# Hybrid SSD and sparse-attention layer: the across decay's matmul joined to the segment sums, all y products one unit later

## The chip, the cores and the metric

The program runs on one core of a Trainium2 chip. The metric is device time in microseconds, the median of several runs. A profile of one execution stands beside it; its lines name engines: PE is TensorE (matmul; PEld its weight loads), DVE is VectorE, ACT is ScalarE, POOL is GpSimd, SPq the queue that issues the DMAs.

## The reference

One decoder layer on x (1, 256, 1024). The input is normalised and modulated, multiplied by one wide matrix `w_in`, and split. One branch is a Mamba-2 SSD scan in two chunks of 128 tokens with 32 heads in 4 groups; the other is a sparse attention with 16 heads. Both are projected, gated, summed, projected again and added to x. The part that the change touches is the SSD scan:

```python
a_cs = jnp.cumsum(adt, axis=2)
seg = a_cs[:, :, :, None] - a_cs[:, :, None, :]
decay = jnp.exp(jnp.where(causal, seg, -jnp.inf))
cb = jnp.einsum('bclgn,bcsgn->bclsg', c_, b_)
y_diag = jnp.einsum('bclsg,bclsgh,bcsghp->bclghp', cb, decay, xdt)
...
y_off = jnp.einsum('bclgn,bcghpn,bclgh->bclghp', c_, prev, jnp.exp(a_cs))
return (y_diag + y_off).reshape(bsz, s, h, p)
```

## The kernel before

**Weight units.** All weights come in units of 128x1024 (512 KB), one DMA each into seven `w_raw` slots. `weight_units` fixes their order (133 of them). For a unit, ACT rounds the raw weights to `w_hi` (L955), DVE and for a part of the columns POOL form `w_lo` = raw - hi (L1230, L1574), and PE runs 8 x 3 matmuls of 256 columns (L727 to L729: hi·hi, hi·lo, lo·hi) into one of three gemm banks in PSUM. ACT and DVE then read the bank out. For the x tiles that is a causal convolution: `conv_acc` on ACT (L988), three taps on DVE (L1277), a tanh on ACT (L997), a gate on DVE (L1239, `x_conv_T`). For z tiles it is a tanh (L962) and a gate (L1239). ACT and DVE prepare weights three units ahead of PE (`AHEAD`). The two `native` matrices w1k and w1v (L703) are used without a split; DVE reads their result at L1299 and L1300 (`cmp_hidden`).

**The order.** `schedule` writes by hand which steps follow which unit: `put(u, step)`. PE and POOL walk through `STEPS`: unit u, then the steps put behind it. ACT and DVE walk through `LATE_STEPS`, in which the steps of unit u stand behind the work of unit u+1. Each engine executes its own list in order, and semaphores tie the lists together. In unit numbers, 13 to 44 are the x and z tiles, four x and four z for each of the SSM groups g; 45 to 49, 52, 55 and 58 are tiles of the attention gate, 50, 51, 53, 54 are w1k, and 56, 57, 59, 60 are w1v. Group g's steps are placed from b = 20 + 8g:

- `xt` (g, c), c = 0, 1: four transposes of the convolved x (L774), which DVE scales to `x_dt` (L1425).
- `seg` i, for each quad i = 2g and 2g+1 of four heads: two matmuls of 512 columns into the score banks (L788); ACT applies relu and exp to each (L1126, L1128: `decay`); DVE (L1432) and POOL (L1624) multiply the two chunks by `cb_T` to `cb_decay`.
- `ea` i: one matmul of 512 columns into a small bank (L793) with the same moving rows; ACT takes the exp (L1133, `decay_across`) and then makes the moving rows of the next quad (L1058, `seg_moving`, four instructions); POOL multiplies by `cb_T` to `cb_decay_across` (L1639).
- `y` i: 12 matmuls with 64 output columns each (L813, L816) into the bank `y_or_o`; DVE adds the skip term in two instructions (L1438) and multiplies by the gate (L1443).
- `ysq` g: ACT squares the group's y (L1140); `ysum` g: POOL adds the squares (L1633, L1634); `ssq`: PE sums them over partitions (L823) and ACT takes the root (L1143), which loads another activation table.

Of the kernel before, what the change touches and what calls it, by code (L numbers as in the profile page):

```python
# [82 lines left out]
def schedule():  # L83

    after = {}

    def put(u, *steps):
        after.setdefault(u, []).extend(steps)

    put(len(PAIRS) - 2, ("ada2", 0))
    put(6, ("dtT", 0))  # L100
    put(7, ("dtA", 0), ("dtE", 0))
    put(8, ("dtB", 0), ("dtL", 0))
    put(10, ("dtC", 0))
    put(13, ("acs", 0))
    for kind in range(3):
        put(15 + kind, ("cb", kind))
    for g in range(SSM_GROUPS):
        b = 20 + 8 * g
        put(b, ("xt", (g, 0)))
        put(b + 1, ("xt", (g, 1)), ("seg", 2 * g))  # L110
        put(b + 2, ("ea", 2 * g))
        put(b + 4, ("y", 2 * g), ("seg", 2 * g + 1))
        put(b + 5, ("ea", 2 * g + 1))
        last = g == SSM_GROUPS - 1
        put(b + 7 + last, ("y", 2 * g + 1))
        put(b + 8 + last, ("ysq", g))
        put(b + 10 + last, ("ysum", g))
    for g in range(KV_GROUPS):
        put(18 + 8 * g, ("blk0", g))
        put(19 + 8 * g, ("blk1", g))  # L120
    put(47, ("clear", 0))
    put(48, ("ssq", 0))
    put(58, ("ssq", 1))
    tiles = TPG * SSM_GROUPS
    w1k, w1v, ks, q, mg = (UNITS.index((kind, 0, 0)) for kind in ("w1k", "w1v", "ks", "q", "mg"))
    norm_units = [w1k + 1, w1k + 2, w1k + 4, w1k + 5, w1v + 1, w1v + 2, w1v + 4, ks + 2, ks + 4, q + 1, q + 3, q + 5]
    norm_units += [mg + n for n in (4, 6, 8, 10, 12, 14)]
    for g, u in enumerate((w1k + 1, w1k + 3, ks + 4, ks + 5)):
        put(u, ("rec", g))
    for j in range(tiles + 2):  # L130
        for ahead, name in ((2, "ynlo"), (1, "ynhi"), (0, "yn")):
            if 0 <= j - ahead < tiles:
                put(norm_units[j], (name, j - ahead))
    at = UNITS.index
    put(at(("w1k", 0, 3)) + 2, ("hidT", 0))
    put(at(("w1v", 0, 3)) + 2, ("hidT", 1))
    put(at(("w1v", 0, 3)) + 1, ("kcp", 0))
    put(at(("w1v", 0, 3)) + 5, ("vcp", 0))
    put(at(("vs", 1, 0)) + 2, ("vt", 0))
    put(at(("w1v", 0, 3)) + 3, ("zero", 0))  # L140
    tiles = [u for u, unit in enumerate(UNITS) if unit[0] != "ag"]
    q7 = tiles.index(at(("q", 7, 0)))

    def after_tile(n, *steps):
        put(tiles[n], *steps)

    after_tile(q7 + 1, ("cs", 0), ("cs", 1))
    after_tile(q7 + 3, ("vt", 1))
    after_tile(q7 + 5, ("ct", 0), ("ct", 1))
    t0 = q7 - 2  # L150
    after_tile(t0 - 3, ("kpos", 0))
    for h in range(ATT_HEADS):
        after_tile(t0 - 2 + 2 * h, ("q2", h))
    for n in range(ATT_HEADS + 2):
        for ahead, name in ((0, "sc"), (2, "pt"), (0, "ex"), (1, "ps")):
            if 0 <= n - ahead < ATT_HEADS:
                after_tile(t0 + 2 * n, (name, n - ahead))
    after_tile(q7 + 2, ("cs2", 0))
    last_h = tiles.index(at(("mg", 15, 0)))
    for p in range(ATT_HEADS // 2):  # L160
        after_tile(t0 + 8 + 4 * p + (p == 0), ("pv", p))
        after_tile(max(last_h + 3, t0 + 8 + 4 * p), ("osp", p))
    put(at(("nsa", 4, 0)), ("agB", 0))
    put(at(("nsa", 6, 0)), ("agB", 1))
    steps = []
    for u in range(len(UNITS)):
        steps.append(("gemm", u))
        steps += after.get(u, [])
    steps += [("flush", 0)]

    late = []
    for u in range(len(UNITS)):
        late += [("gemm", u)] + after.get(u - 1, [])
    late += [("flush", 0)] + after.get(len(UNITS) - 1, [])
    return steps, late


STEPS, LATE_STEPS = schedule()
SPLIT_IDX, NATIVE_IDX, TILE_IDX = {}, {}, {}
for _u, (_kind, _j, _part) in enumerate(UNITS):  # L180
# [1611 lines left out]
```

## Time and profile before

| | us |
|---|---|
| median of 3 runs | 454.94 |
| lowest and highest | 454.66 to 456.67 |
| the profiled execution | 455.79 |
| its span in the trace | 454.0 |
| PE busy | 435.1 (96%) |
| DVE busy | 346.3 (76%) |
| ACT busy | 281.5 (62%) |
| POOL busy | 205.6 (45%) |

Times in the views are microseconds from the start of the span. Matmuls are pipelined: the profiler's durations overlap, and the distance between two starts is what one costs in a stream. "Idle before" is the time in which an engine stood still ahead of a group, with what ended it. The granted clock (PEclk) is the share of TensorE's full clock that the chip allowed.

### The profile page before, as it was taken

How to read it: one execution, taken by the hardware profiler on the slowest of the kernel's cores; microseconds unless marked ns; L12 is line 12 of the kernel's file. 1: busy time of each engine (PE TensorE's matmuls, PEld its weight loads, DVE VectorE, ACT ScalarE, POOL GpSimd, SP SyncE). 2: the span in 40 equal slices, each digit the busy share in tenths (PEclk: the TensorE clock that was granted, in tenths of full speed). 3: DMA queues.
4: the chain of work that ended last, by engine and by line, in shares of the span. 5: the costliest groups of instructions: out<-in, count | busy, mean ns of one | idle time of the engine just before them, and what ended most of it. 6: DMA issues, size and time to landing. Idle time of an engine off the chain costs nothing.

```text
span 454.0 us, 9851 instructions
## 1 busy us (share of the span) xinstructions
PE 435.1 (96%) x3638; PEld 400.5 (88%) x3638; DVE 346.3 (76%) x615; ACT 281.5 (62%) x560; POOL 205.6 (45%) x195
## 2 busy tenths in 40 slices
PE   2899999999999999999899999999999999999995
PEld 2597999999999999986899999999989899999873
DVE  0366889999999999468788879478668888787633
ACT  3245885878687986656898647476557554544441
POOL 0147661533346436735483444355443653355430
PEclk9999999999999999999999969999999999999999
DMA  7999636474535436168756442424344364497002
GB/s 283 420 415 397 210 135 186 139 232 141 171 110 167 158 141 184 49 198 274 266 190 214 160 140 95 139 93 152 129 160 165 140 244 176 170 385 249 33 0 92
DMA packets 22391, 84.04 MB, mean 185 GB/s; under 512 B 2492, under 2 KB 2882, under 8 KB 21186
## 3 DMA queue, kind: packets, MB, share of 16 engines
q1 hardware_dynamic: 22344, 83.42, 52.6%
q8 instruction: 29, 0.48, 0.4%
q14 instruction: 18, 0.15, 0.1%
HBM read 82.36 MB, written 1.05 MB: 184 GB/s over the span
## 4 chain that ended last, share of the span: by engine, by line
PE 50%; DVE 1%; issue 0%; ACT 0%; DVEq 0%
PE gemm L727 12%; PE gemm L729 11%; PE gemm L728 11%; PE y_or_o L933 3%; PE score L897 1%; PE score L899 1%; PE small L871 1%; PE score L900 1%; PE small L652 1%; PE small L654 1%; PE score L654 1%; PE score L653 1%; PE small L653 1%; PE score L652 1%; PE small L909 1%; PE small L915 1%
## 5 line engine op out<-in xcount | busy, mean ns | idle before, releaser
L1574 POOL TENSOR_TENSOR w_lo<-w_raw,w_hi 128x256 fp32r<-128x256 f32 x89 | 116.0, 1307 | 159.1 <-ACT w_hi L955 150.6
L727 PE MATMUL gemm<-h_hi,w_hi 128*128 128x256 f32 x600 | 171.5, 286 | 2.1 <-DVE cmp_hidden L1300 1.2
L729 PE MATMUL gemm<-h_hi,w_lo 128*128 128x256 f32 x600 | 167.8, 280 | 0.0
L728 PE MATMUL gemm<-h_lo,w_hi 128*128 128x256 f32 x600 | 167.8, 280 | 0.0
L1230 DVE TENSOR_TENSOR w_lo<-w_raw,w_hi 128x768 fp32r<-128x768 f32 (+1 forms) x117 | 128.1, 1098 | 42.8 <-ACT w_hi L955 42.3
L955 ACT CAST w_hi<-w_raw 128x1024 fp32r<-128x1024 f32 x117 | 122.2, 1045 | 44.8 <-PE gemm L729 25.2
L727 PEld LDWEIGHTS gemm<-h_hi,w_hi 128*128 128x128 f32 x600 | 114.1, 190 | 5.9 <-issue 3.0
L728 PEld LDWEIGHTS gemm<-h_lo,w_hi 128*128 128x128 f32 x600 | 114.3, 191 | 0.8 <-issue 0.2
L729 PEld LDWEIGHTS gemm<-h_hi,w_lo 128*128 128x128 f32 x600 | 113.9, 190 | 0.0
L727 PE MATMUL gemm<-ynorm_hi,w_hi 128*128 128x256 f32 x128 | 36.1, 282 | 0.0
L729 PE MATMUL gemm<-ynorm_hi,w_lo 128*128 128x256 f32 x128 | 35.4, 276 | 0.0
L728 PE MATMUL gemm<-ynorm_lo,w_hi 128*128 128x256 f32 x128 | 35.4, 276 | 0.0
L1624 POOL TENSOR_TENSOR cb_decay<-decay,cb_T 128x512 f32<-128x512 f32 x8 | 14.5, 1816 | 44.7 <-ACT decay L1128 39.1
L1277 DVE SCALAR_TENSOR_TENSOR conv_acc<-gemm,conv_half,conv_acc 128x255 f32<-128x255 f32 (+2 forms) x66 | 31.6, 479 | 3.0 <-ACT conv_acc L988 1.3
L1188 ACT ACTIVATE probs<-score,softmax_small 128x128 f32<-128x128 f32 (+1 forms) x64 | 26.1, 422 | 11.3 <-DVE softmax_small L1493 11.3
L727 PEld LDWEIGHTS gemm<-ynorm_hi,w_hi 128*128 128x128 f32 x128 | 24.0, 188 | 0.7 <-issue 0.7
L728 PEld LDWEIGHTS gemm<-ynorm_lo,w_hi 128*128 128x128 f32 x128 | 24.1, 188 | 0.0
L729 PEld LDWEIGHTS gemm<-ynorm_hi,w_lo 128*128 128x128 f32 x128 | 24.0, 188 | 0.0
L1195 ACT COPY probs_T<-small 128x512 f32<-128x512 f32 x16 | 9.4, 590 | 23.1 <-PE y_or_o L933 21.6
L988 ACT ACTIVATE conv_acc<-gemm,conv_half 128x256 f32<-128x256 f32 x22 | 12.4, 565 | 16.2 <-DVE x_conv_T L1239 8.7
L962 ACT ACTIVATE tanh_tmp<-gemm 128x256 f32<-128x256 f32 x24 | 9.1, 380 | 16.2 <-PE gemm L729 15.3
L727 PE MATMUL gemm<-o_hi,w_hi 128*128 128x256 f32 x64 | 18.8, 294 | 0.0
(253 smaller groups left out, 893.0 us busy)
## 6 DMA issues: line engine op xcount, KB each, us to landing
w_raw<-in_wpack SPq DMA_DIRECT2D x133, 512.0 KB, 3.7
w_ada_shift_scale<-in_w_ada SPq DMA_DIRECT2D x8, 1024.0 KB, 15.5
x_T<-in_xT SPq DMA_DIRECT2D x2, 512.0 KB, 5.9
x_residual<-in_x_tok SPq DMA_DIRECT2D x1, 1024.0 KB, 6.1
out_tok_dram<-out_tok SPq DMA_DIRECT2D x4, 256.0 KB, 2.1
ada_gate_products<-in_gate_bias SPq DMA_DIRECT2D x1, 512.0 KB, 4.0
g_post_rows<-in_g_post_rows SPq DMA_DIRECT2D x1, 512.0 KB, 5.7
consts<-in_consts SPq DMA_DIRECT2D x1, 272.0 KB, 22.0
```

The costliest lines, as they stand in the source:

```text
L727: nc.tensor.matmul(bank[:, 0:SEQ], w_hi, hi[:, k0 + k, :], start=first, stop=False)
L728: nc.tensor.matmul(bank[:, 0:SEQ], w_hi, lo[:, k0 + k, :], start=False, stop=False)
L729: last = nc.tensor.matmul(bank[:, 0:SEQ], w_lo, hi[:, k0 + k, :], start=False, stop=end)
L933: last = nc.tensor.matmul(bank[64 * k:64 * k + 64, P * kt:SEQ], V[:, b, kt, g, :], src, start=False, stop=(b == 1 and kt == 1), skip_group ...
L955: nc.scalar.copy(WH[:, n % HI_SLOTS, :], RAW[:, u % RAW_SLOTS, :]).then_inc(hi_ready, 1)
L988: nc.scalar.activation(ACC[:, ci % 2, :], bank, ACT.Identity, bias=CW[:, 96 + col:97 + col], scale=CW[:, 4 * col + 3:4 * col + 4]).then_in ...
L1188: last = nc.scalar.activation(E[:, k, b, P * qt:P * qt + nk], SB[qt][:, nk * b:nk * b + nk], ACT.Exp, bias=SM[:, k, 0, c:c + 1], accum_out ...
L1195: nc.scalar.copy(PT[:, i % 2, :, 0:SEQ], bank[:, :].rearrange("p (b q) -> p b q", b=2)).then_inc(release, 1)
L1230: nc.vector.tensor_tensor(WL[:, n % LO_SLOTS, 0:c], RAW[:, u % RAW_SLOTS, 0:c], WH[:, n % HI_SLOTS, 0:c], ALU.subtract).then_inc(lo_ready, 1)
L1277: ins = nc.vector.scalar_tensor_tensor(ACC[:, ci % 2, s:SEQ], bank[:, 0:SEQ - s], CW[:, 4 * col + tap:4 * col + tap + 1], ACC[:, ci % 2, s ...
L1574: nc.gpsimd.tensor_tensor(WL[:, n % LO_SLOTS, c:1024], RAW[:, u % RAW_SLOTS, c:1024], WH[:, n % HI_SLOTS, c:1024], ALU.subtract).then_inc( ...
L1624: nc.gpsimd.tensor_tensor(MM[:, 1, :, :], EX[:, 1, :, :], CB[:, 1, i // 2, :].unsqueeze(1).to_broadcast([P, 4, P]), ALU.mult).then_inc(mm_ ...
```

## The change

The steps of a group are put elsewhere; nothing else is touched.

```diff
@@ -107,12 +107,11 @@
         b = 20 + 8 * g
         put(b, ("xt", (g, 0)))
-        put(b + 1, ("xt", (g, 1)), ("seg", 2 * g))
-        put(b + 2, ("ea", 2 * g))
-        put(b + 4, ("y", 2 * g), ("seg", 2 * g + 1))
-        put(b + 5, ("ea", 2 * g + 1))
+        put(b + 1, ("xt", (g, 1)))
+        put(b + 2, ("seg", 2 * g), ("ea", 2 * g))
+        put(b + 5, ("y", 2 * g), ("seg", 2 * g + 1), ("ea", 2 * g + 1))
         last = g == SSM_GROUPS - 1
-        put(b + 7 + last, ("y", 2 * g + 1))
+        put(b + 8, ("y", 2 * g + 1))
         put(b + 8 + last, ("ysq", g))
```

A group's first `seg` goes from behind unit b+1 to behind b+2, where its `ea` already was. The first `y` and the second `seg` go from b+4 to b+5, where the second `ea` was. The second `y` goes from b+7 to b+8, which is also the place of the next group's first `xt`; in the last group it was at b+8 before. The file is one line shorter, so that line numbers behind it are one less.

In the queue of PE at the end of a group, before: the second y stands between two weight units (the last rows of one and the first row of the next are shown), and the transposes come a unit later.

```order
L729 MATMUL gemm<-h_hi,w_lo 128x256
L813 MATMUL y_or_o<-cb_decay,x_dt 64x128 x4
L816 MATMUL y_or_o<-cb_decay_across,x_dt 64x128 x2
L813 MATMUL y_or_o<-cb_decay,x_dt 64x128 x4
L816 MATMUL y_or_o<-cb_decay_across,x_dt 64x128 x2
L727 MATMUL gemm<-h_hi,w_hi 128x256
```

The same place after:

```order
L728 MATMUL gemm<-h_hi,w_lo 128x256
L812 MATMUL y_or_o<-cb_decay,x_dt 64x128 x4
L815 MATMUL y_or_o<-cb_decay_across,x_dt 64x128 x2
L812 MATMUL y_or_o<-cb_decay,x_dt 64x128 x4
L815 MATMUL y_or_o<-cb_decay_across,x_dt 64x128 x2
L773 MATMUL small<-consts,x_conv_T 128x128 x4
L726 MATMUL gemm<-h_hi,w_hi 128x256
```

The unit between the y and the transposes (L773, before L774) now stands ahead of the y.

In the queue of ACT in the first half of a group, from the cast ahead of the decay to the cast behind the next tile, before: the decay of quad 2g, a convolution tile with its cast, then the exponential for `ea` and the moving rows.

```order
L955 CAST w_hi<-w_raw 128x1024
L1126 ACTIVATE decay<-score 128x512
L1128 ACTIVATE decay<-decay 128x512
L1126 ACTIVATE decay<-score 128x512
L1128 ACTIVATE decay<-decay 128x512
L988 ACTIVATE conv_acc<-gemm,conv_half 128x256
L997 ACTIVATE tanh_tmp<-conv_acc 128x256
L955 CAST w_hi<-w_raw 128x1024
L1133 ACTIVATE decay_across<-small 128x512
L1058 ACTIVATE seg_moving<-acs_rows,consts 128x2x128 x4
L988 ACTIVATE conv_acc<-gemm,conv_half 128x256
```

The same place after:

```order
L987 ACTIVATE conv_acc<-gemm,conv_half 128x256
L996 ACTIVATE tanh_tmp<-conv_acc 128x256
L954 CAST w_hi<-w_raw 128x1024
L1125 ACTIVATE decay<-score 128x512
L1127 ACTIVATE decay<-decay 128x512
L1125 ACTIVATE decay<-score 128x512
L1127 ACTIVATE decay<-decay 128x512
L1132 ACTIVATE decay_across<-small 128x512
L1057 ACTIVATE seg_moving<-acs_rows,consts 128x2x128 x4
L987 ACTIVATE conv_acc<-gemm,conv_half 128x256
```

The decay has moved behind one more convolution tile and is followed at once by the exponential and the moving rows. In the second half of a group the same two blocks have come together around a z tile.

In the queue of ACT ahead of the `w1k` units, before: the last decay, the root for `ssq` with its two table loads, a tanh, the last exponential, the cast.

```order
L1126 ACTIVATE decay<-score 128x512
L1128 ACTIVATE decay<-decay 128x512
L1143 ACT_TABLE_LOAD
L1143 ACTIVATE rstd_y_102<-small,eps_columns 128x512
L962 ACT_TABLE_LOAD
L962 ACTIVATE tanh_tmp<-gemm 128x256
L1133 ACTIVATE decay_across<-small 128x512
L955 CAST w_hi<-w_raw 128x1024
```

The same place after:

```order
L1142 ACT_TABLE_LOAD
L1142 ACTIVATE rstd_y_102<-small,eps_columns 128x512
L961 ACT_TABLE_LOAD
L961 ACTIVATE tanh_tmp<-gemm 128x256
L1125 ACTIVATE decay<-score 128x512
L1127 ACTIVATE decay<-decay 128x512
L1125 ACTIVATE decay<-score 128x512
L1127 ACTIVATE decay<-decay 128x512
L1132 ACTIVATE decay_across<-small 128x512
L954 CAST w_hi<-w_raw 128x1024
```

The last decay has moved behind the root and the tanh.

## Rows read from the trace of the kernel before

**Rows 1.** Waits of PE: engine, line, what for; us, times, longest.

```profile
PE gemm L727 <- DVE cmp_hidden L1300: 1.2, 1, 1.2
...
PE gemm L703 <- DVE cmp_hidden L1300: 0.7, 1, 0.7
```

**Rows 2.** Stretches: window, length, busy by engine (count), granted clock, DMA share, GB/s.

```profile
core 0: us, PE busy (x) PEld busy (x) DVE busy (x) ACT busy (x) POOL busy (x), PEclk, DMA share, GB/s
120.24:147.94 27.70, 27.70 (x258) 26.84 (x256) 26.64 (x42) 21.63 (x40) 12.95 (x10) 1.00 0.47 151
...
265.30:272.20 6.90, 6.90 (x35) 6.81 (x34) 4.19 (x8) 2.25 (x6) 2.29 (x3) 0.51 0.48 150
```

**Rows 3.** PE in order of time: start, us, engine, line, operation, count.

```profile
106.89 0.28 PE L727 MATMUL gemm<-h_hi,w_hi 128*128 128x256 f32 x1
...
109.72 0.39 PE L793 MATMUL small<-seg_moving,acs_cols 128*128 128x512 f32 x1
109.95 0.28 PE L727 MATMUL gemm<-h_hi,w_hi 128*128 128x256 f32 x1
...
112.67 0.28 PE L727 MATMUL gemm<-h_hi,w_hi 128*128 128x256 f32 x1
...
116.63 0.39 PE L816 MATMUL y_or_o<-cb_decay_across,x_dt 128*64 128x128 f32 x4
116.95 0.38 PE L727 MATMUL gemm<-h_hi,w_hi 128*128 128x256 f32 x1
...
120.24 0.37 PE L727 MATMUL gemm<-h_hi,w_hi 128*128 128x256 f32 x1
...
129.75 0.28 PE L727 MATMUL gemm<-h_hi,w_hi 128*128 128x256 f32 x1
...
140.37 0.28 PE L727 MATMUL gemm<-h_hi,w_hi 128*128 128x256 f32 x1
...
199.94 0.39 PE L816 MATMUL y_or_o<-cb_decay_across,x_dt 128*64 128x128 f32 x4
200.16 1.90 PE L703 MATMUL gemm<-w_raw,cmp_blocks 128*60 128x256 f32 x16
```

**Rows 4.** ACT in order of time, in the group from 120.24.

```profile
121.30 1.06 ACT L1140 ACTIVATE y_sq<-z_gate_then_y 128x1024 f32<-128x1024 f32 x1
...
124.66 0.59 ACT L1126 ACTIVATE decay<-score 128x512 f32<-128x512 f32 x1
...
126.99 0.57 ACT L988 ACTIVATE conv_acc<-gemm,conv_half 128x256 f32<-128x256 f32 x1
...
128.71 0.59 ACT L1133 ACTIVATE decay_across<-small 128x512 f32<-128x512 f32 x1
...
130.79 0.56 ACT L988 ACTIVATE conv_acc<-gemm,conv_half 128x256 f32<-128x256 f32 x1
```

**Rows 5.** DVE, and one row of POOL, in order of time, in the same group.

```profile
130.40 2.31 DVE L1230 TENSOR_TENSOR w_lo<-w_raw,w_hi 128x1024 fp32r<-128x1024 f32 x1
132.64 1.50 DVE L1277 SCALAR_TENSOR_TENSOR conv_acc<-gemm,conv_half,conv_acc 128x255 f32<-128x255 f32 x3
...
134.39 1.22 DVE L1230 TENSOR_TENSOR w_lo<-w_raw,w_hi 128x1024 fp32r<-128x1024 f32 x1
135.53 1.51 DVE L1277 SCALAR_TENSOR_TENSOR conv_acc<-gemm,conv_half,conv_acc 128x255 f32<-128x255 f32 x3
...
130.15 1.48 POOL L1639 TENSOR_TENSOR cb_decay_across<-decay_across,cb_T 128x512 f32<-128x512 f32 x1
```

**Rows 6.** PE, ACT and DVE ahead of the read of the w1k bank.

```profile
187.96 0.66 PE L813 MATMUL y_or_o<-cb_decay,x_dt 128*64 128x128 f32 x8
...
193.67 0.39 PE L793 MATMUL small<-seg_moving,acs_cols 128*128 128x512 f32 x1
...
189.96 0.60 ACT L1126 ACTIVATE decay<-score 128x512 f32<-128x512 f32 x1 [0.57 <-PE score L788]
...
197.52 1.22 DVE L1230 TENSOR_TENSOR w_lo<-w_raw,w_hi 128x768 fp32r<-128x768 f32 x1 [1.00 <-ACT w_hi L955]
...
205.32 0.42 DVE L1300 TENSOR_TENSOR cmp_hidden<-gemm,cmp_hidden 60x256 f32<-60x256 f32 x1
```

## The prediction, made before the changed kernel ran

> **What bounds the kernel now.** I read what TensorE (PE) waits for, then the engines' busy time by stretches. In the 27.7 us of the second SSM group PE is busy 27.70, with VectorE (DVE) at 26.64 and ScalarE (ACT) at 21.63 [rows 2]. The three groups that start at 92.53, 120.24 and 147.94 read alike. Of all waits of PE only two of size lie near the change, 0.7 and 1.2 us, both for `cmp_hidden` L1300 on DVE, behind the SSM stage [rows 1]. So in the stage that is edited PE waits for nobody, and a change can pay in three ways only: fewer or cheaper PE instructions, another pace of the ones there are, or an effect on those two waits.
>
> PE's starts in time order give the pace. Matmuls are pipelined, so I use distances of starts, not durations. A weight unit is 24 matmuls. Behind `seg` (L788) a unit runs from 106.89 to 109.72, 2.83 us; after `ea` (L793, 109.72) the next one runs from 109.95 to 112.67, 2.72 us [rows 3]. The same unit thus has two paces, 118 and 113 ns a matmul, and each holds until something other than a unit comes between. In the trace a single `ea` is followed by the fast pace 7 times of 7 where a unit follows it, `seg` by the slow one 7 of 7, the `y` matmuls by the slow one 3 of 3, transposes by the fast one.
>
> **The change, part by part.** No instruction is added or removed. What moves are borders on PE, and whole blocks in the queues of ACT, DVE and GpSimd (POOL).
>
> *Merged borders.* The odd `y` (1, 3, 5) now stands directly ahead of the next group's first transposes; before, a unit lay between. A `y` that ends before a unit costs two steps: 116.63 to 116.95 (0.32 us for the last four, where four otherwise take 0.22, as at 199.94 to 200.16, where the native matmuls follow), and then a first matmul recorded at 0.38 us, 0.10 above the others' 0.28 [rows 3]. The second is gone, since the matmul behind the transposes pays such a step already (0.37 at 120.24 [rows 3]). If the first goes as well, a border saves 0.21, otherwise 0.10 to 0.11. I take 0.11: the nearest row for a `y` followed by full-width work is the 0.32 one. Three borders: -0.33 us, and -0.65 as the other end.
> The Trainium skill, TensorEngine Tiling (Array Packing), Key Properties, says that a change of tiling mode drains TensorE. The `y` matmuls fill 64 columns, as the native ones do with 60, and the transposes fill 128: by that rule the 0.32 step stays and the merge is worth 0.11, not 0.21; the trace's 0.22 before the native matmuls and 0.32 before a unit agree.
> The other borders come out even: `ea` costs 0.23 us between units (109.72 to 109.95), and a 512-column matmul behind another takes about the same, so joining it to `seg` saves nothing by itself; `seg` behind a unit instead of behind transposes is spared the first step of 0.1 that the unit behind the transposes then pays.
>
> *Pace.* Ten units run slow because `seg` or `y` stands ahead of them: in groups 0 to 2 those at the places b+2, b+5 and b+8 of each group, and one in group 3. In the new order `seg` and `y` stand directly ahead of no unit; `ea` or transposes do (`ssq` once, as before). If the last instruction sets the pace, all ten gain 2.83 - 2.72 = 0.11: -1.1 us. What no row shows is `ea` directly behind `seg`. If it keeps the slow pace of `seg`, then the six units that follow the two joined places of each group run slow, three of which stood so before; with the shorter last group some 20 instead of 10: +1.1. Both ends stay in the range. I take -1.1, because the instruction that stands directly ahead is the one behind which all seven fast units begin.
>
> *ACT's queue.* Before, the four passes of the decay (124.66 to 126.99, 2.33 us) and the `ea` exponential with the four rows for the next quad (128.71 to 130.79, 2.08 us) had a convolution tile and a weight cast between them [rows 4]. Now they are one stretch of 4.4 us, and the next tile's `conv_acc` stands behind it, so DVE, which needs it, can run dry. I walk group 1 with T=0 at the end of the z unit that closes group 0. PE: `y` and transposes to 1.7, units end at 4.6, 7.9; `seg`, `ea` to 8.6; units end at 11.3, 14.1, 17.0; `y`, `seg`, `ea` to 19.2; then 22.0, 24.7, 27.4. ACT begins the third convolution tile at about 14.0, DVE at 14.5, 3.2 us behind PE's end of that tile; before it was 132.64 against 129.75, 2.9 [rows 3, 5]. So the new gap is filled for the most part by the lag that DVE has anyway.
> What that lag may cost: DVE's taps on one bank began at 135.53 and took 1.51; PE writes the bank again from 140.37 [rows 3, 5], a slack of 3.4 us. In my walk the thinnest such slack is 1.2 to 2 us. Also `y_sq` on ACT now waits for `y` of the same slot, and holds the next `conv_acc` behind it: 1.06 of it [rows 4] and 0.5 of the tile against 0.7 us of DVE's own work, 0.85 us of DVE idle per group, as much as DVE has free (27.70 - 26.64 = 1.06). Cost on PE: 0, with +1.0 us as the other end.
> First the row: a `w_lo` of 1.22 us takes 2.31 where a POOL multiply of 1.48 started 0.25 us ahead of it [rows 5]. The Trainium skill, SBUF — State Buffer, SBUF: two separate sides, calls the pair of ports that the two engines share an exclusive lock. The new place of the POOL multiplies decides which DVE operation they meet; by my walk one of the two meets DVE's new idle time.
>
> *The two waits behind.* PE's 0.7 and 1.2 us end when DVE has read the `w1k` and `w1v` banks. From the `w_lo` at 197.52 to the read at 205.32 DVE works without a gap, and that `w_lo` had waited 1.00 us for ACT's cast [rows 6]. ACT works through from 189.96 to there: the last decay, two table loads with the root between, a tanh, the exponential, the cast. In the new order the root stands one unit ahead of the last decay, and the decay one unit later. PE's unit behind it ended at 193.67, where `ea` begins [rows 6]; take out the `y` and `seg` that left (187.96 to 189.99, 2.03) and the 1.4 saved so far, and it ends at 190.2. Then `y` 1.5, and ACT begins the decay 2.0 us behind the start of `y`, as now (187.96 to 189.96): 192.3; plus 2.4, 0.5 and 1.05, cast done at 196.2 against 197.5. So 1.3 of the 1.4 us comes through, and everything from there to the end shifts with it, as PE has no other wait of size.
>
> **Sum.** -0.33 - 1.1 = -1.4 on PE, of which 1.3 us passes. The profiled execution took 455.79 us for a span of 454.0; that gives 454.5. The runs' median is 454.94, 0.85 below the profiled one, and with the same 1.3 taken off it the time is 453.6 us.
>
> **Rivals.**
> 1. *The slow pace stays* behind the joined `seg` and `ea`: +1.1 - 0.33 = +0.8, thus 455.7. For it: `seg` and `ea` have the same shape, and the second `seg` matmul did not cure the slow pace either. Against: `ea` always did. A half of it (one of the two joined places fast) gives 454.6.
> 2. *DVE becomes the bound*, on the other side. Place: the gemm banks in the x tiles of groups 1 and 2. Per group DVE works 26.64 us and would gain 0.85 idle behind `y_sq`, 0.7 to 1.8 behind ACT's stretch and 1.1 where the port lock hits: 29.0 to 30 against PE's 27.3, so up to 1.7 to 2.2 us of lag a group. It decides once three groups have used up the 3.4 us of slack: 5.1 - 3.4 = 1.7 us of PE waiting, the fast pace lost with it: 454.94 - 0.33 + 1.7 = 456.3, slower than before. Against: ACT's stretch hangs on PE's `seg`, so most of the lag is taken up again at each group's third tile.
> 3. *The change does nothing on PE*: pace and borders are tied to the instructions, not to their order: 454.9.
> 4. *The half clock*. From 265.3 to 272.2 us the granted clock was 0.51, the 1.2 GHz level, with PE busy all 6.90 of them [rows 2], and none of its waits of size stands near [rows 1], so idleness did not cause it. If the shift moves it away, some 3.4 us go (451.5); a second one adds as much (458).
> The Trainium skill, TensorE: Matmul & The Clock Gate, What's actually happening, has the clock fall to 1.2 GHz after an idle window; by it this stretch would not be there at all, and the time would be 451.5; the trace disagrees.
>
> **How the numbers follow.** Forecast 453.6: 0.50. One joined place fast, or nothing on PE (454.6 to 454.9): 0.18. Slow pace (455.7): 0.13. DVE bound (456.3, up to 457.5): 0.12. Clock away 0.03, second half-clock stretch 0.04. The range 452.4 to 456.5 reaches from the 0.65 of the borders with all of the pace and a shorter DVE chain to the middle of the DVE case, and leaves out under 0.2. A measurement of this kernel tells 0.5% (2.3 us) from no change, so below 452.7 is faster and above 457.2 slower: faster 0.09 (the clock, the low end), same 0.83, slower 0.08.
>
> **What would show it.** Right: the units behind `ea` at all eight joined places take 2.72 us; the odd `y` has the transposes behind it and one 0.2 us step fewer; a group takes 27.3 us instead of 27.7; DVE starts a group's third convolution tile about 3 us behind PE; the last decay on ACT begins near 192.3 and `cmp_hidden` L1300 ends about 1.3 us earlier. Wrong: units of 2.83 us behind the joined places; PE waits for `conv_acc` L1276 or `x_conv_T` between 120 and 190; another count or place of half-clock stretches.

## The result: slower, by a little less than two microseconds

| | before | changed |
|---|---|---|
| median of 20 runs, us | 455.1 | 457.1 |
| lowest and highest | 454.27 to 456.92 | 455.99 to 458.81 |
| profiled execution | 455.79 | 457.48 |
| span | 454.0 | 455.7 |

The ratio is 1.0036, with a 95% interval of 1.0026 to 1.0046, so +1.6 us (1.2 to 2.1); the two medians lie 2.0 apart. The forecast of 453.6 and the range up to 456.5 were both wrong, and the sign too.

PE's waits in the changed kernel (engine, tile and line, what for; total, times, longest), which answer to [rows 1]:

```profile
PE gemm L726 <- DVE conv_acc L1276: 1.3, 1, 1.3
PE gemm L726 <- DVE cmp_hidden L1299: 1.1, 1, 1.1
...
PE gemm L702 <- DVE cmp_hidden L1299: 1.0, 1, 1.0
PE y_or_o L812 <- DVE cb_decay L1431: 1.0, 2, 0.7
...
PE small L792 <- DVE x_dt L1424: 0.2, 1, 0.2
```

Two kinds are new: the `y` matmuls wait for `cb_decay`, the last `ea` for `x_dt`. (The 1.3 us for `conv_acc` lies near 66 us, ahead of everything that was moved. It is 0.7 in the trace of before, and takes either size in two executions of one program, below.)

The stretches of the three groups and the start of the fourth, with the columns of [rows 2]:

```profile
93.89:121.24 27.35, 27.35 (x257) 26.49 (x256) 24.86 (x40) 21.90 (x40) 9.61 (x8) 1.00 0.51 159
121.24:148.93 27.69, 27.51 (x257) 26.60 (x256) 26.00 (x40) 20.61 (x38) 10.81 (x9) 1.00 0.46 149
148.93:177.81 28.88, 27.92 (x257) 26.56 (x256) 26.95 (x43) 21.52 (x40) 11.33 (x10) 1.00 0.41 131
177.81:191.11 13.30, 13.09 (x109) 12.37 (x107) 9.78 (x17) 8.28 (x17) 9.90 (x11) 1.00 0.56 193
```

Against 27.7 us in each group before, the first one does what was predicted (27.35), the second has lost the gain (27.69), and the third is 1.2 us longer than before (28.88). Something builds up. From the unit behind the first transposes to the end of that part of the program (unit start 92.53 to 224.85 before, 93.89 to 227.76 after) the changed kernel takes 133.87 us, before took 132.32: +1.55, which is the measured difference. The 1.36 us by which it starts later at 93.89 belongs to that one execution: over the 14 profiles of this document this start lies anywhere from 92.39 to 93.89. The spans differ by 1.7 only, because the two profiles have half-clock stretches of different length behind this part; the last section has their price.

**Where the wait arises.** A `y` needs two kinds of product: `cb_decay`, which VectorE makes for one chunk and GpSimd for the other, and `cb_decay_across` from GpSimd. In front of a `y`, three rows stand: VectorE's product `cb_decay`, GpSimd's `cb_decay_across`, and PE's first `y` matmul. Before, second `y` of the second group (DVE, POOL, PE in order of time):

```profile
140.13 0.68 DVE L1432 TENSOR_TENSOR cb_decay<-decay,cb_T 128x512 f32<-128x512 f32 x1
...
140.78 1.53 POOL L1639 TENSOR_TENSOR cb_decay_across<-decay_across,cb_T 128x512 f32<-128x512 f32 x1 [1.11 <-ACT decay_across L1133]
...
143.19 0.55 PE L813 MATMUL y_or_o<-cb_decay,x_dt 128*64 128x128 f32 x6
```

The last product ends at 142.31, `y` starts at 143.19: 0.88 us to spare. The same `y` after, and one of the next group:

```profile
143.46 0.87 DVE L1437 SCALAR_TENSOR_TENSOR x_conv_T<-x_conv_T,params,y_or_o 128x256 f32<-128x256 f32 x2
144.36 0.89 DVE L1442 TENSOR_TENSOR z_gate_then_y<-x_conv_T,z_gate_then_y 128x512 f32<-128x512 f32 x1
145.17 1.78 DVE L1431 TENSOR_TENSOR cb_decay<-decay,cb_T 128x512 f32<-128x512 f32 x1
...
144.86 1.54 POOL L1638 TENSOR_TENSOR cb_decay_across<-decay_across,cb_T 128x512 f32<-128x512 f32 x1 [0.16 <-ACT decay_across L1132]
...
147.05 0.66 PE L812 MATMUL y_or_o<-cb_decay,x_dt 128*64 128x128 f32 x8 [0.18 <-issue]
...
165.11 0.33 PE L812 MATMUL y_or_o<-cb_decay,x_dt 128*64 128x128 f32 x2 [0.72 <-DVE cb_decay L1431]
```

`cb_decay` takes 1.78 us instead of 0.68, because POOL's `cb_decay_across` now runs at the same time: it started 0.31 us earlier and ends at 146.40, and the DVE operation ends 0.55 us behind that, at 146.95. PE starts 0.10 later. The Trainium skill, SBUF — State Buffer, SBUF: two separate sides, says that of a VectorE operation with two SBUF inputs and a GpSimd one, whichever starts first holds the shared ports to its end and the other is blocked; these rows agree.

The second ingredient is the square of y on ACT, which in the new order has the same place as the `y` that it needs, where it stood one unit behind it before (start, length, in brackets the idle time before it). With it, the operation of DVE that starts late for it:

```profile
125.84 1.06 ACT L1139 ACTIVATE y_sq<-z_gate_then_y 128x1024 f32<-128x1024 f32 x1 [4.91 <-DVE z_gate_then_y L1442]
126.81 0.54 ACT L987 ACTIVATE conv_acc<-gemm,conv_half 128x256 f32<-128x256 f32 x1
...
127.39 1.52 DVE L1276 SCALAR_TENSOR_TENSOR conv_acc<-gemm,conv_half,conv_acc 128x255 f32<-128x255 f32 x3 [0.98 <-ACT conv_acc L987]
```

PE had finished that convolution tile at 124.16. Before, the square stood at 121.30 [rows 4], ahead of the tile, and delayed nothing. Now ACT stands 4.91 us for DVE's gate, and DVE then stands 0.98 us for ACT, here and again at 156.46 in the third group.

The next table has two things. The first is the slack: how much every `y` has to spare (start of `y` less the end of the later of the two kinds of product, us; 0.10 behind DVE and 0.26 behind POOL mean that `y` waited or was about to). The second is the lag: how far DVE is behind PE (start of a group's first `x_dt` less the start of the unit behind the transposes).

| | y 0 | 1 | 2 | 3 | 4 | 5 | 6 | 7 | lag of x_dt, four groups |
|---|---|---|---|---|---|---|---|---|---|
| before | 1.88 | 1.50 | 0.92 | 0.88 | 0.94 | 0.89 | 0.98 | 0.87 | 3.56, 2.35, 2.81, 2.93 |
| changed | 2.20 | 1.49 | 0.33 | 0.10 | 0.10 | 0.10 | 1.57 | 0.59 | 3.16, 4.48, 5.86, 6.11 |

### The profile page after: what moved, and what is told of

Read it like the earlier page. It is cut to its first block, busy times and chain, and to the rows that moved or that the text cites. A ratio compares the mean times of both kernels' runs of the same rounds, so it can differ in the third digit from the quotient of the medians.

```text
span 455.7 us, 9851 instructions
## 1 busy us (share of the span) xinstructions
PE 433.7 (95%) x3638; PEld 397.7 (87%) x3638; DVE 347.7 (76%) x615; ACT 280.4 (62%) x560; POOL 202.5 (44%) x195
## 4 chain that ended last, share of the span: by engine, by line
PE 41%; DVE 5%; ACT 3%; issue 2%; DVEq 0%; ACTq 0%
PE gemm L726 10%; PE gemm L728 9%; PE gemm L727 9%; PE y_or_o L932 3%; DVE w_lo L1229 2%; ACT w_hi L954 1%; PE score L898 1%; PE score L896 1%; PE small L651 1%; PE small L653 1%; PE score L653 1%; PE score L652 1%; PE small L652 1%; PE score L651 1%; PE y_or_o L926 1%
## 5 line engine op out<-in xcount | busy, mean ns | idle before, releaser
L1229 DVE TENSOR_TENSOR w_lo<-w_raw,w_hi 128x768 fp32r<-128x768 f32 (+1 forms) x117 | 125.1, 1072 | 42.4 <-ACT w_hi L954 42.0
L1623 POOL TENSOR_TENSOR cb_decay<-decay,cb_T 128x512 f32<-128x512 f32 x8 | 11.4, 1426 | 39.7 <-ACT decay L1127 30.2
L727 PE MATMUL gemm<-o_lo,w_hi 128*128 128x256 f32 x64 | 17.8, 278 | 0.0
```

The costliest lines, as they stand in the source:

```text
L727: nc.tensor.matmul(bank[:, 0:SEQ], w_hi, lo[:, k0 + k, :], start=False, stop=False)
L1229: nc.vector.tensor_tensor(WL[:, n % LO_SLOTS, 0:c], RAW[:, u % RAW_SLOTS, 0:c], WH[:, n % HI_SLOTS, 0:c], ALU.subtract).then_inc(lo_ready, 1)
L1623: nc.gpsimd.tensor_tensor(MM[:, 1, :, :], EX[:, 1, :, :], CB[:, 1, i // 2, :].unsqueeze(1).to_broadcast([P, 4, P]), ALU.mult).then_inc(mm_ ...
```

## The experiments

Each ratio is to the kernel before, timed on the same chip, with its 95% interval. Theory A blames the square, which holds the next group's first convolution tile. Theory B blames ACT's joined stretch of decay, exponential and moving rows. Theory C blames the lock of the ports that VectorE and GpSimd share. The later runs test the slack theory (a `y` has about 0.9 us to spare, and the change uses it up), and VectorE's load.

**1. The square one unit later.**

```diff
-        put(b + 8 + last, ("ysq", g))
-        put(b + 10 + last, ("ysum", g))
+        put(b + 9, ("ysq", g))
+        put(b + 11, ("ysum", g))
```

> The changed kernel, with the square of the group's y (ACT) and its sums (POOL) one unit later, as far behind the second y as before the change. Theory A, the square on ACT holds the next group's first convolution tile: in the changed kernel it waits 4.9 us for VectorE's gate, and VectorE then stands 0.98 us for conv_acc in every group. Here ACT's wait goes, PE's waits for conv_acc and cb_decay between 140 and 180 us go, the groups take 27.4 us, and the time is 453.7 to 454.3. Theory B, ACT's joined stretch of decay, exponential and moving rows: the time stays at 456.5 to 457.1. Theory C, the lock between VectorE and GpSimd (cb_decay 1.78 us instead of 0.68 to 1.10): also 456.5 to 457.1.

Ratio 0.9998 (0.9984 to 1.0012), median 455.38. The whole loss is back, but the gain that theory A expected (453.7 to 454.3) is not there. Theories B and C, which expected no change against 457.1, fail as the only cause. The groups, ACT's square and the one wait that is left:

```profile
92.39:119.75 27.36, 27.36 (x258) 26.50 (x256) 25.61 (x41) 21.89 (x40) 10.13 (x9) 1.00 0.50 163
119.75:147.18 27.43, 27.43 (x257) 26.57 (x256) 26.76 (x39) 20.85 (x39) 11.44 (x9) 1.00 0.45 152
147.18:175.38 28.20, 27.82 (x257) 26.83 (x256) 27.26 (x43) 21.46 (x39) 11.68 (x10) 1.00 0.44 135
```

```profile
153.01 1.06 ACT L1139 ACTIVATE y_sq<-z_gate_then_y 128x1024 f32<-128x1024 f32 x1 [1.21 <-DVE z_gate_then_y L1442]
...
173.51 0.33 PE L812 MATMUL y_or_o<-cb_decay,x_dt 128*64 128x128 f32 x2 [0.38 <-DVE cb_decay L1431]
```

Two groups now hold 27.4; the third still breaks, with DVE busy 27.26 of 28.20 and `cb_decay` at 1.78 us. Theory A is right and is not all of it.

**2 to 4. One part of the change alone.** Only the second `y`:

```diff
-        put(b + 7 + last, ("y", 2 * g + 1))
+        put(b + 8, ("y", 2 * g + 1))
```

> The kernel before, with only the second y of each group one unit later, in the place of the square. Theory A: this part alone brings the wait of the square, so 455.8 to 457.0. Theories B and C, which blame the joined seg and ea: 454.8 to 455.1, a merged border of 0.05 to 0.11 us per group being too small to see.

Only the first segment sum:

```diff
-        put(b + 1, ("xt", (g, 1)), ("seg", 2 * g))
-        put(b + 2, ("ea", 2 * g))
+        put(b + 1, ("xt", (g, 1)))
+        put(b + 2, ("seg", 2 * g), ("ea", 2 * g))
```

> The kernel before, with only the first segment sum of each group one unit later, next to its ea. Theory A: nothing waits, the unit that ran at 2.83 us behind the segment sum runs at 2.72, four times 0.11, so 454.5 to 454.9. Theory B: 455.4 to 456, since ACT's stretch of 4.4 us now stands ahead of the third convolution tile. Theory C: likewise 455.3 to 456, with a cb_decay of 1.78 us on VectorE.

Only the middle:

```diff
-        put(b + 4, ("y", 2 * g), ("seg", 2 * g + 1))
-        put(b + 5, ("ea", 2 * g + 1))
+        put(b + 5, ("y", 2 * g), ("seg", 2 * g + 1), ("ea", 2 * g + 1))
```

> The kernel before, with only the first y and the second segment sum one unit later, next to the second ea. Theory A: the unit behind them turns fast, four times 0.11, so 454.5 to 454.9, and nothing waits. Theory B: 455.3 to 456 from ACT's stretch around the first z tile. In all theories the last decay of group 3 comes one unit later on ACT and the cast ahead of w1k with it.

Ratios 1.0020 (1.0007 to 1.0033), 1.0025 (1.0008 to 1.0042) and 1.0029 (1.0013 to 1.0044). The medians are 456.07, 456.63 and 456.45, so each part alone is slower than before by 0.9 to 1.3 us, and each has new waits of `y`. One PE row of each, in the order of the three kernels:

```profile
189.34 0.40 PE L813 MATMUL y_or_o<-cb_decay,x_dt 128*64 128x128 f32 x3 [0.90 <-POOL cb_decay_across L1639]
```

```profile
106.53 0.66 PE L813 MATMUL y_or_o<-cb_decay,x_dt 128*64 128x128 f32 x8 [1.07 <-POOL cb_decay_across L1639]
```

```profile
144.20 0.66 PE L812 MATMUL y_or_o<-cb_decay,x_dt 128*64 128x128 f32 x8 [0.67 <-DVE cb_decay L1431]
```

The first is theory A's: in its third group ACT waits 4.0 us ahead of its square, the decay behind it starts 2.65 us behind its segment sum instead of 1.25, and `y` waits for what follows from it. The fourth group, to which the row belongs, shows the same chain. In the other two no square was moved. Both shorten the way from one segment sum of a group to its `y` from three units to two, and with 0.9 us to spare that is too much. Theory A had expected nothing to wait in them, and both times lie above the 456 at which the brackets of B (and of C, for the first) end; these are misses. They led to the theory of the slack. They are not parts of the loss that could be added up: the whole change moves each `y` along with its segment sum and leaves three units between them, so the shortened way of these two kernels is not in it. They do show that ACT's joined stretch has a price on DVE: in experiment 3 DVE stands 1.39 us for `conv_acc` at 134.80.

**5, 7 and 8. The product that holds the ports, cut.** In the changed kernel, in the one of experiment 1, and as a control in the kernel before. These three leave out 120 of the 128 columns a head of `cb_decay_across` for quads 1 to 7, so their y is not the layer's y; they are only there for their times:

```diff
-                    nc.gpsimd.tensor_tensor(CE[:], EA[:], CB[:, 2, g, :].unsqueeze(1).to_broadcast([P, 4, P]),
+                    w = P if i == 0 else 8
+                    nc.gpsimd.tensor_tensor(CE[:, :, 0:w], EA[:, :, 0:w], CB[:, 2, g, 0:w].unsqueeze(1).to_broadcast([P, 4, w]),
```

> The changed kernel with GpSimd's product cb_decay_across cut to 8 of its 128 columns a head for quads 1 to 7 (left out: the rest of that product, so the across term of y is that of quad 0). VectorE's cb_decay, which took 1.78 us beside it and 0.68 alone, is then alone. In the changed kernel y waits for VectorE's cb_decay with a slack of 0.10 us four times. Theory slack (the product chain segment sum, decay, product, y has about 0.9 us to spare in the kernel before, and the change eats it by the lock and by lag): 455.3 to 455.9, PE's waits for cb_decay gone or under 0.3 us. Theory square alone: 456.8 to 457.3, since ACT still waits for the gate in every group.

> The changed kernel with both cures: the square one unit later, and cb_decay_across cut to 8 columns a head for quads 1 to 7 (the rest is left out). Theory slack with both causes: PE waits nowhere between 92 and 190 us, groups of 27.4 us, 453.7 to 454.3. If something third holds it (VectorE's own 26.6 to 27.3 us of work a group as a bound): 455.0 to 455.5, as with the square moved alone.

> Control: the kernel before with the same product cut to 8 columns a head for quads 1 to 7 (the rest is left out). All theories: the time of before, 455.0 to 455.4, since no y waits there (slack 0.9 to 1.9 us), unless the shorter work shifts the two waits for cmp_hidden by some tenths.

Ratios 0.9995 (0.9979 to 1.0012), 0.9978 (0.9965 to 0.9991) and 1.0003 (0.9988 to 1.0019): 455.05, 454.01, 455.6 us. Groups two and three of the run with both cures, and one of the control:

```profile
120.53:147.96 27.43, 27.43 (x257) 26.57 (x256) 25.52 (x42) 21.70 (x39) 9.06 (x10) 1.00 0.45 155
147.96:175.39 27.43, 27.43 (x257) 26.57 (x256) 25.34 (x42) 21.75 (x39) 10.06 (x10) 1.00 0.46 153
```

```profile
121.14:148.84 27.70, 27.70 (x258) 26.84 (x255) 25.93 (x43) 21.82 (x40) 10.67 (x10) 1.00 0.47 153
```

With the product small, `cb_decay` of the middle groups takes 0.74 us in the fifth run, no `y` waits in it even though the square still stands in its bad place, and the groups take 27.4. DVE's lag still grows (3.56, 4.40, 5.14, 6.16), but every `y` keeps 0.73 us or more: the lag and the lengthened product make PE wait together, not the lag alone. The control shows that the cut alone is worth nothing to PE in the groups, while DVE's work in a group falls from 26.64 [rows 2] to 25.93. (Behind the groups, PE's first wait for `cmp_hidden` is 0.4 us in all three instead of the 0.7 of before [rows 1].) The slack theory is borne out: the seventh run lies where it said, the fifth 0.3 us below; the control's median is 0.2 above its bracket, with a ratio of one.

**6 and 10. The kernel before, with `y`, square and sums moved together.**

```diff
-        put(b + 7 + last, ("y", 2 * g + 1))
-        put(b + 8 + last, ("ysq", g))
-        put(b + 10 + last, ("ysum", g))
+        put(b + 8, ("y", 2 * g + 1))
+        put(b + 9, ("ysq", g))
+        put(b + 11, ("ysum", g))
```

> The kernel before, with the second y of each group one unit later and its square and sums one unit later too; seg and ea stay apart. Against the run with the odd y alone (456.07, two waits of PE for cb_decay_across of 0.9 and 0.7 us, with GpSimd's sums of squares standing ahead of that product): theory slack: the sums now stand behind the product, both waits go, and the time is 454.2 to 454.8. If only the joining of seg and ea costs: 454.8 to 455.2. If a later y costs by itself: 455.8 and more.

> The kernel before with the second y, the square and the sums one unit later, measured a second time. Its trace was 0.56 us shorter than before between the first group and 225 us, while the timed runs were 0.14 us apart with an interval of 0.7 either way. Theory slack: 454.5 to 454.8. If the trace's gain is given back later: 455.0 to 455.3.

Ratios 0.9997 (0.9981 to 1.0013) and 0.9992 (0.9976 to 1.0008). The waits of experiment 2 are gone and the groups take 27.5. The medians are 455.30, above the 454.2 to 454.8 of the slack theory, and 454.75, within its 454.5 to 454.8. Both ratios are below one and neither is clear of it; a gain of the 0.5 us that the traces have (0.55 and 0.47 us up to 225) is compatible with both, and not shown by them.

**9 and 11. With `ea` apart, next to the joined form.**

```diff
-        put(b + 2, ("seg", 2 * g), ("ea", 2 * g))
-        put(b + 5, ("y", 2 * g), ("seg", 2 * g + 1), ("ea", 2 * g + 1))
+        put(b + 2, ("seg", 2 * g))
+        put(b + 3, ("ea", 2 * g))
+        put(b + 5, ("y", 2 * g), ("seg", 2 * g + 1))
+        put(b + 6, ("ea", 2 * g + 1))
```

> The changed kernel with the square and its sums one unit later and each ea put one unit behind its seg again (seg b+2, ea b+3, y and seg b+5, ea b+6, y b+8, square b+9): the order before, moved by one unit, without the joining. Theory slack and lock: VectorE's cb_decay takes 0.68 to 1.2 us instead of 1.78, every y has 0.5 us or more to spare, PE does not wait between 92 and 190 us, groups take 27.4 to 27.5 us, and the time is 454.1 to 454.7, below the joined form (455.4). If joining as such is harmless and VectorE's whole work is the bound: 455.2 to 455.6, like the joined form.

> The changed kernel with the square and its sums one unit later, measured a second time next to the form with seg and ea apart. Theory slack and lock: VectorE's cb_decay of 1.78 us stays, y waits once for 0.4 us in the third group, 455.0 to 455.5, above the form with ea apart by 0.5 or more.

Ratios 1.0013 (1.0002 to 1.0024) and 1.0006 (0.9992 to 1.0020): 456.17 and 455.9 us. Both are misses: the first was expected at 454.1 to 454.7, and the second 0.5 us or more above it, where their intervals overlap. The first is the useful one. Taking the products apart did not help. Its second and third group, and a wait:

```profile
120.07:147.95 27.88, 27.55 (x258) 26.64 (x256) 27.11 (x43) 21.65 (x39) 11.97 (x11) 1.00 0.45 140
147.95:176.21 28.26, 27.55 (x258) 26.64 (x256) 27.81 (x42) 21.70 (x39) 12.66 (x11) 1.00 0.44 145
```

```profile
163.79 0.66 PE L814 MATMUL y_or_o<-cb_decay,x_dt 128*64 128x128 f32 x8 [0.71 <-POOL cb_decay_across L1640]
```

DVE is busy 27.81 of 28.26 us. Separated, POOL's operations meet other ones of DVE: a `w_lo` takes 2.31 us at 134.05, and a `cb_decay` still takes 1.78 at 159.91, now beside POOL's work on the squares. So joining is not the fault in itself; VectorE has no room for a PE that wants a group in 27.4 us.

**12. VectorE relieved, the whole layer computed.** To experiment 1:

```diff
-        put(18 + 8 * g, ("blk0", g))
+        put((18, 45, 46, 47)[g], ("blk0", g))
```

> The whole layer, nothing left out: the changed kernel with the square and its sums one unit later, and VectorE's four small additions for the key blocks (cmp_blocks, 1.4 to 1.5 us a group) of groups 1 to 3 taken out of the SSM groups and put behind units 45, 46 and 47, where VectorE idles. Theory VectorE bound (26.6 to 27.3 us of work a group, much of it stretched by GpSimd, against 27.4 on PE): VectorE's lag behind PE no longer grows, no y waits for cb_decay, groups take 27.4 us, 453.9 to 454.5, like the run with both cures that left work out. If the product chain alone is too short and VectorE's load is not the cause: the 0.4 to 0.7 us wait for cb_decay in the third group stays, 455.0 to 455.6.

Ratio 0.9976 (0.9962 to 0.9990), median 454.55 against 455.56. The three groups, and two of the moved blocks at their new place on DVE:

```profile
92.72:120.15 27.43, 27.43 (x258) 26.57 (x255) 25.57 (x40) 21.90 (x40) 10.45 (x9) 1.00 0.50 162
120.15:147.58 27.43, 27.43 (x257) 26.57 (x256) 24.66 (x39) 21.70 (x39) 11.97 (x11) 1.00 0.45 153
147.58:175.01 27.43, 27.43 (x257) 26.57 (x256) 24.68 (x40) 21.70 (x39) 12.09 (x10) 1.00 0.46 152
```

```profile
184.68 3.75 DVE L522 TENSOR_TENSOR cmp_blocks<-kv_cmp_T,params 64x120 f32<-64x120 f32 x4
...
188.91 1.30 DVE L522 TENSOR_TENSOR cmp_blocks<-kv_cmp_T,params 64x120 f32<-64x120 f32 x4
```

PE waits nowhere between 92 and 191 us, as theory had it, and the time is within 0.05 us of its bracket. Every `y` has 0.87 us or more to spare (1.92, 1.49, 2.31, 1.24, 2.26, 1.37, 5.11, 0.87) and the lag of `x_dt` no longer grows (3.54, 2.92, 3.19, 2.58). Yet `cb_decay` still takes 1.78 us where it meets POOL, and DVE still stands 1.4 us behind ACT's joined stretch (at 133.12): theories B and C each name something real, which costs PE nothing once DVE has room. This version, whose y is complete, is faster than both kernels: the change's order plus two cures that it needed.

## Why the prediction was wrong, step by step

- **What bounds the kernel**: right that PE waited for nobody, wrong in what I took for its nearest follower. I measured DVE's distance at the gemm banks (3.4 us) and never the distance at `y`, which has two producers. It was 0.9 us (0.88 in the rows above). Experiments 3 and 4 show how thin that is: with one unit less between segment sum and `y`, PE waits at once. The change itself takes no unit away (except from the last `y`); in it the 0.9 us goes to the lag and to the longer product. I had also said that the three groups read alike. For PE they do, but DVE, whose 26.64 us I took from the second, is busier in the other two of the kernel before:

```profile
92.53:120.24 27.71, 27.71 (x258) 26.86 (x256) 27.27 (x45) 20.89 (x39) 11.05 (x9) 1.00 0.55 177
...
147.94:175.64 27.70, 27.70 (x258) 26.85 (x256) 27.04 (x43) 21.74 (x40) 14.39 (x12) 1.00 0.44 144
```

So it had 0.4 to 0.7 us free there, not 1.06, less than the 0.85 us of new idleness that I set against it.
- **Pace, -1.1**: the direction was right. The first unit behind joined `seg` and `ea` took the fast 2.72 to 2.73 us in 39 of 42 cases (seven in each of the six traces with that order), 2.83 in three; so rival 1, which had it slow there, did not happen. But the rule on the instruction directly ahead was not. Units behind a lone second `seg`, slow in 3 of 3 in the kernel before, were fast in 3 of 3 in experiment 2, in the first group with the same order on PE up to there. And the unit behind the merged `y` and transposes, fast before, was slow in experiment 12 in 3 of 3 (2.91 us with its first step of 0.2, where 2.82 was forecast). Ten units gained and three lost: seven by 0.11 is 0.8.
- **Merged borders, -0.33**: measured 0.05 each instead of 0.11. The 0.32 step stayed, as taken: the 24 matmuls of a `y` take 1.46 us ahead of transposes as ahead of a unit. The four transposes behind `y` take 0.41 us (148.52 to 148.93) instead of the 0.36 that they took behind a unit (119.88 to 120.24 [rows 3]), so half of the saved step comes back. In experiment 12, where nothing waits, PE's part came to 131.44 - 132.32 = -0.88 us up to 225 us instead of -1.4.
- **ACT's and DVE's queues, 0 with +1.0 as the other end**: this is the step that failed, and it decided the sign. The pieces were seen, each near its size (idle behind the square 0.85 forecast, 0.98 measured; the lock 1.1 forecast, 1.1 measured on `cb_decay`), and then set at nothing against the wrong slack, the 3.4 us at the gemm banks instead of the 0.9 us at `y`. In my walk DVE began the third convolution tile 14.5 us behind T, the end of the group before; it was 135.87 - 119.37 = 16.5. Against the trace of experiment 12 the changed kernel loses 83.92 - 82.29 = 1.6 us in three groups and 0.8 behind them, the greater part in waits: -0.9 + 2.4 = +1.5. So this term was about +2.4 where the forecast had 0.
- **Rival 2**, VectorE as the bound, 456.3 to 457.5 at a chance of 0.12, is nearest to what happened, and its upper part holds the time. That the time fits is partly luck, since the place was off: the waits stand at `y`, not at the banks, so they began in the second group and not once three groups had used up 3.4 us. Its sum was off too: 26.64 with 0.85, 0.7 to 1.8 and 1.1 is 29.3 to 30.4, thus 2.0 to 3.1 us of lag a group where I wrote 1.7 to 2.2; the lag column grew by 1.3, 1.4 and 0.25. Against it I had argued that DVE takes up its lag in each group's third tile. In the changed kernel it does not.
- **The two waits behind**: the step held where it could be seen. In experiment 12 the last decay on ACT began at 193.02, and `cmp_hidden` L1299 started at 204.72 instead of 205.32, 0.8 us earlier counted from the first group (92.72 and 92.53), against PE's 0.8. In the changed kernel the decay came at 196.34, since PE brought a loss.
- **Half clock**: the stretch is tied neither to the order nor to the shift, and its price was mis-sized: a stretch as long as the one of before costs 1.2 us of the whole time, not 3.4, see below.

What is not settled: why a block of units runs at 113 or 118 ns a matmul, how the loss divides between the square, the lock and VectorE's load (moving the square alone, or cutting the product alone, brings the time back to that of before; only two cures together bring a gain), and whether the order of experiments 6 and 10 gains anything.

## What to carry to other kernels

When PE never waits, list for every kind of instruction on PE how long its latest producer had been done, and take the smallest, not the one of the largest stream: that slack, less what the change takes from it, says whether a gain on PE comes through. A second engine at 96% of a loop period turns a gain of 1% on the first into a lag that adds up and shows only some turns later, so the first turn proves nothing. If a step waits for another engine, place it where its input is surely ready: here moving a square by one slot was worth about 1.6 us of the 2.7 that lie between the changed kernel and experiment 12's.

## What the runs showed of the hardware that was not expected

**The half-clock stretch comes and goes in one program.** Experiments 6 and 10 are the same kernel. The same 11 us of both (columns as in [rows 2], the granted clock third from the end):

```profile
262.00:273.00 11.00, 10.96 (x67) 10.46 (x66) 7.46 (x17) 4.39 (x14) 4.41 (x6) 0.69 0.43 144
```

```profile
262.00:273.00 11.00, 11.00 (x95) 10.53 (x94) 7.72 (x18) 5.12 (x15) 4.61 (x7) 1.00 0.44 144
```

67 matmuls against 95, with PE busy throughout in both. The stretch at 1.2 GHz was in 7 of the 14 profiles. In four of them (before, experiments 6, 8, 12) it is 6.8 us long, in three (the changed kernel, experiments 2 and 11) 3.4 us. Between the units at 259.4 and at 270.3 to 273.6 the long one cost 3.2 us, but most of that is made up later. From the unit that ends the moved part (224.85 in before) to the end of the span it is 229.15 to 229.27 us in the four profiles with the long stretch, and 227.92 to 227.95 in all ten others, whether they have the short one or none. So the long stretch costs 1.2 us of the whole and the short one nothing. The timed runs of the kernel before say the same: 34 of them have a mean granted clock of 0.990 to 0.992, as the long stretch gives (0.991 in the profile of before), and take 456.2 us on average; another 80 have a higher one and take 455.0. How the rest of the 3.2 us is made up is not shown. The Trainium skill, TensorE: Matmul & The Clock Gate, What's actually happening, gives an idle window as the cause; neither run has one there, so the traces still disagree.

**Two paces in one program.** Experiments 1 and 11 are the same kernel too. The third group's first unit behind joined `seg` and `ea`, and the start of the next:

```profile
153.97 0.28 PE L726 MATMUL gemm<-h_hi,w_hi 128*128 128x256 f32 x1
...
156.80 0.28 PE L726 MATMUL gemm<-h_hi,w_hi 128*128 128x256 f32 x1
```

```profile
154.31 0.28 PE L726 MATMUL gemm<-h_hi,w_hi 128*128 128x256 f32 x1
...
157.04 0.28 PE L726 MATMUL gemm<-h_hi,w_hi 128*128 128x256 f32 x1
```

2.83 and 2.73 us for the same 24 matmuls. What stands ahead makes a pace likely, not certain. Likewise PE's step near 65 us that ends with its wait for `conv_acc`, ahead of everything that was changed, was 1.60 us in one of these two and 0.99 in the other, so a single pair of traces has to be compared from the place of the change on, not from zero.
